# Routing logits and norm sums inside the output projection, and a gather for four experts at a time

## The reference

```python
x = x + merged @ w_out[l]
x = x + expert_choice_ffn(rms_norm(x, norm_ffn[l]), router[l], exp_gate[l], exp_up[l], exp_down[l])

def expert_choice_ffn(h, router, w_gate, w_up, w_down):
    cap = CAPACITY_FACTOR * S // N_EXPERTS                       # 2 * 256 // 16 = 32
    aff = jax.nn.softmax(jnp.einsum('bsd,de->bse', h, router), axis=-1)
    vals, idx = lax.top_k(aff.transpose(0, 2, 1), cap)
    xg = jax.vmap(lambda hb, ib: hb[ib])(h, idx)
    hid = jax.nn.silu(jnp.einsum('becd,edf->becf', xg, w_gate)) * jnp.einsum('becd,edf->becf', xg, w_up)
    y = jnp.einsum('becf,efd->becd', hid, w_down) * vals[..., None]
    return ...                                                   # y added at the chosen tokens
```

## Time and profile before

| | us |
|---|---|
| median of 3 runs | 1902.39 (1899.36 to 1904.59) |
| the profiled execution | 1904.66 |
| its span | 1902.9 |
| PE busy in the span | 1573.6 (83%) |
| weight load busy | 1152.3 (61%) |
| DVE busy | 549.2 (29%) |
| ACT busy | 259.3 (14%) |
| DMA | 405.39 MB, 213 GB/s over the span |

### The profile page before, as it was taken

One profiled execution on the slowest core, in us unless ns is written; L12 is line 12 of the kernel. 1 busy time (PEld: TensorE's weight loads), 2 busy tenths in 40 slices (PEclk: granted clock), 3 DMA queues, 4 the chain that ended last, 5 costly groups with the idle time before them and its releaser, 6 DMA issues.

```text
span 1902.9 us, 25312 instructions
## 1 busy us (share of the span) xinstructions
PE 1573.6 (83%) x11140; PEld 1152.3 (61%) x11140; DVE 549.2 (29%) x1199; ACT 259.3 (14%) x618; POOL 72.0 (4%) x96
## 2 busy tenths in 40 slices
PE   7979999998879999999878879998866656666666
PEld 4857788886637888878656657776732222222223
DVE  3670444301132311033647554323220000000002
ACT  2330100002212000001323222220100000000001
POOL 0120000000000000000110111200000000000000
PEclk8989999998979999999988999999988787778787
DMA  8466578744343644333100001323629999999992
GB/s 359 155 258 248 218 279 318 278 142 155 133 155 121 236 151 155 138 128 133 68 24 24 2 24 45 114 108 126 250 87 421 422 420 421 421 421 420 419 421 105
DMA packets 57485, 405.39 MB, mean 213 GB/s; under 512 B 6168, under 2 KB 8344, under 8 KB 8864
## 3 DMA queue, kind: packets, MB, share of 16 engines
q1 hardware_dynamic: 53984, 390.35, 52.5%
q10 hardware_dynamic: 3392, 13.42, 1.8%
HBM read 402.69 MB, written 1.06 MB: 212 GB/s over the span
## 4 chain that ended last, share of the span: by engine, by line
PE 65%; DMA 23%; DVE 9%; ACT 2%; issue 1%; POOL 0%; ACTq 0%; SPq 0%; POOLq 0%; DVEq 0%
PE bank L409 63%; DMA weight_ring<-weights 22%; DVE arena L1499 3%; PE bank L416 2%; DVE arena L1505 2%; ACT arena L1151 1%; DVE arena L1502 1%; DVE arena L1830 1%; DVE rstd L1555 1%; DVE normed_T L1505 0%; DMA arena<-x 0%; DVE rstd L1897 0%; DVE arena L1692 0%; DVE arena L1828 0%; ACT normed_T L1151 0%
## 5 line engine op out<-in xcount | busy, mean ns | idle before, releaser
L409 PE MATMUL bank<-normed_T,weight_ring 128*128 128x256 f32 x2640 | 608.1, 388 | 27.0 <-ACT arena L1151 12.4
L409 PEld LDWEIGHTS bank<-normed_T,weight_ring 128*128 128x128 f32 x2640 | 504.5, 194 | 108.1 <-ACT arena L1151 18.0
L409 PE MATMUL bank<-weight_ring,arena 128*32 128x256 f32 (+1 forms) x2976 | 270.0, 484 | 146.9 <-DMA weight_ring<-weights 138.5
L409 PE MATMUL bank<-arena,weight_ring 128*128 128x256 f32 x1456 | 329.6, 384 | 9.7 <-ACT arena L1151 6.8
L409 PEld LDWEIGHTS bank<-arena,weight_ring 128*128 128x128 f32 x1456 | 279.5, 193 | 51.0 <-issue 8.5
L409 PEld LDWEIGHTS bank<-weight_ring,arena 128*32 128x32 f32 (+1 forms) x2976 | 100.7, 132 | 302.9 <-DMA weight_ring<-weights 206.5
L1151 ACT ACTIVATE arena<-bank 128x256 f32<-128x256 f32 (+4 forms) x299 | 109.9, 374 | 1171.2 <-PE bank L409 625.1
L409 PE MATMUL bank<-arena 64*64 64x64 f32 (+7 forms) x3096 | 225.7, 283 | 28.4 <-DVE arena L1499 14.1
L409 PEld LDWEIGHTS bank<-arena 64*64 64x64 f32 (+5 forms) x3096 | 167.3, 155 | 97.5 <-issue 48.6
L1505 DVE SCALAR_TENSOR_TENSOR arena<-arena,bank 128x256 f32<-128x256 f32 x141 | 59.4, 422 | 544.1 <-PE bank L409 276.4
L416 PE MATMUL bank<-packed_consts,arena 128*128 128x128 f32 (+1 forms) x166 | 42.8, 358 | 65.1 <-DVE arena L1502 35.6
(11 more groups left out here) (119 smaller groups left out, 637.5 us busy)
## 6 DMA issues: line engine op xcount, KB each, us to landing
weight_ring<-weights SPq DMA_DIRECT2D x370, 1024.0 KB, 10.2
arena<-ahead ACTq DMA_DIRECT2D x8, 1024.0 KB, 18.0
packed_consts<-packed ACTq DMA_DIRECT2D x1, 2852.0 KB, 13.6
arena<-bias_by_distance ACTq DMA_DIRECT2D x2, 1024.0 KB, 7.0
arena<-x SPq DMA_DIRECT2D x1, 1024.0 KB, 5.2
out<-arena SPq DMA_DIRECT2D x2, 512.0 KB, 2.6
packed_consts<-packed SPq DMA_DIRECT2D x1, 254.5 KB, 2.8
bias_by_distance<-arena ACTq DMA_DIRECT2D x1, 16.0 KB
```

Source lines behind the costliest of these rows:

```text
L409: return e.matmul(out, lhsT, rhs, start=start, stop=stop, skip_group_check=True)
```

## The change

- w_out is written out with `route_sums(n)` after the next block. DVE no longer waits for the norm: after each residual block it multiplies it by the norm's weight alone (`ts`) into hT. ACT's squares go to an area `sq8` of their own. `route_sums` makes four products for a block: two of 16 columns (logits of the tokens of each half, not yet divided by the norm) and two of one column (sums of squares per token).
- The norm is now a number per token on its partition. ACT takes the root of two 128x1 columns, loads the table of the exponential, and takes the exponentials with the reciprocal of the root as scale; the copies to htok multiply by it too.
- PE's transposes of hT come after w_out; three of the four clears of accumulators come between the transposes of the affinities and the places, the fourth after the gather.
- DVE's first round of the top tokens reads the bank directly; the copies and the subtraction of 1 go, and the iota starts at 1.
- The selection is made for a group of four experts at a time (128 columns). Group 0 is gathered before the experts, with 16 products of 128 columns, into B[2] and B[3]; group g + 1 in two halves of 8 products into B[3], after the mixes of the second and the third expert of group g, with an ACT copy each. `gsel` goes; `g4` is computed for each expert from places and affinities.

The lines added, with a little around them (what is removed stands in the functions above):

```diff
 EXPERTS, CAP = 16, 32
+BATCH = 4
+BATCHES = EXPERTS // BATCH
...
+ROUTE_PE = {"sum": 2, "aff": 3, "place": 4}
+ROUTE_V = {"bias": 1, "aff": 2, "place": 3, "select": 4}
...
+        self.sel = a.take(NT * EXPERTS * CAP)
+        self.xg = [a.take(KD * BATCH * CAP) for _ in range(2)]
+        self.sq8 = area[:, NT * D:NT * D + KD * T]
+        self.aff, self.post, self.st = a.take(NT * EXPERTS), a.take(NT * EXPERTS), a.take(6 * NT)
+        self.wk, self.mk, self.ps_ = [a.take(T)[0:EXPERTS, :] for _ in range(3)]
...
+        self.zeros = a.take(P)
...
+        a = Arena(area, n, a.at)
...
+    def route_sums(n):
+
+        e.wait_ge(s.normed, 8 * NORM_FFN2 + n + 1)
+        for j in range(NT):
+            ins = mm(B[6 + j][:, 0:EXPERTS], hT[:, n, j * P:(j + 1) * P], m.col("router", n * EXPERTS, EXPERTS), n == 0, n == KD - 1)
+            if n == KD - 1:
+                ins.then_inc(s.route_pe, 1)
+        e.wait_ge(s.square, squares_before(NORM_FFN2) + n + 1)
+        for j in range(NT):
+            ins = mm(B[4 + j][:, 0:1], m.sq8[:, n * T + j * P:n * T + (j + 1) * P], m.ones[:, 0:1], n == 0, n == KD - 1)
+        if n == KD - 1:
+            ins.then_inc(s.sumsq, 1)
+
+    for n in range(KD):
         if n < 4:
             e.wait_ge(s.branch_out, 2 * KD + n + 5)
...
+        else:
+            e.wait_ge(s.xT, 8 * NORM_FFN2 + n - 3)
+        for k in range(KD):
+            if n == 0:
+                e.wait_ge(s.merged, k + 1)
+            w = feed.tile("w_out_2", k, n)
+            if k < KD - 1:
+                fed(B[n % 4][:, 0:T], w, m.mg[:, k, :], k == 0, False)
+            else:
+                mm(B[n % 4][:, 0:T], w, m.mg[:, k, :], False, True).then_inc(s.res, 1)
+        if n:
+            route_sums(n - 1)
+    route_sums(KD - 1)
...
     e.wait_ge(s.xT, 8 * NORM_FFN2 + KD)
...
+    e.wait_ge(s.route_v, ROUTE_V["aff"])
+    e.wait_ge(s.root, NORM_FFN2 + 1)
     for j in range(NT):
         ins = flip(B[4][0:EXPERTS, j * P:(j + 1) * P], m.aff[:, j * EXPERTS:(j + 1) * EXPERTS])
     ins.then_inc(s.route_pe, 1)
...
+    e.wait_ge(s.zeroed, ZEROED["experts"])
+    for j in range(1, 4):
+        mm(B[4 + j][:, :], m.zeros, m.hT_[:, 0:512], True, False)
+    e.wait_ge(s.route_v, ROUTE_V["place"])
     for j in range(NT):
         ins = flip(B[4][:, j * EXPERTS:(j + 1) * EXPERTS], m.ps_[:, j * P:(j + 1) * P])
     ins.then_inc(s.route_pe, 1)
...
+
+    def gather(g, k, out):
+
+        for j in range(NT):
+            at = j * EXPERTS * CAP + g * BATCH * CAP
+            ins = mm(out, m.htok[:, j, k * P:(k + 1) * P], m.sel[:, at:at + BATCH * CAP], j == 0, j == NT - 1)
+        return ins
+
+    e.wait_ge(s.route_v, ROUTE_V["select"])
     e.wait_ge(s.h_tok, 2 * NT)
...
+    for half in range(2):
+        for k in range(4):
+            ins = gather(0, 4 * half + k, B[2 + half][:, k * P:(k + 1) * P])
         ins.then_inc(s.x_sum, 1)
...
+    e.wait_ge(s.route_v, ROUTE_V["select"] + 1)
+    mm(B[4][:, :], m.zeros, m.hT_[:, 0:512], True, False)
     for x in range(EXPERTS):
...
+        g, y = x // BATCH, x % BATCH
+        xg = [m.xg[g % 2][:, k * P + y * CAP:k * P + (y + 1) * CAP] for k in range(KD)]
+        if y == 0:
+            e.wait_ge(s.x_out, 2 * g + 2)
         if x:
             e.wait_ge(s.e_act, x)
         quarters(B[0], f"exp_gate{x}", lambda k: xg[k]).then_inc(s.e_gate, 1)
...
+        e.wait_ge(s.x_out, 2 * g + 2 + max(0, y - 1) * (g + 1 < BATCHES))
...
+        if y in (1, 2) and g + 1 < BATCHES:
+            e.wait_ge(s.route_v, ROUTE_V["select"] + g + 1)
+            for k in range(4):
+                ins = gather(g + 1, 4 * (y - 1) + k, B[3][:, k * P:(k + 1) * P])
+            ins.then_inc(s.x_sum, 1)
...
     e.wait_ge(s.o_out, 2 * n_items)
     for c in range(AHEAD):
         e.dma_start(m.ahead[:, c * TPC * P:(c + 1) * TPC * P], dram["ahead"][c]).then_inc(s.ahead[c], 16)
...
+    for n in range(KD):
+        e.wait_ge(s.xT, 8 * NORM_FFN2 + n + 1)
+        act(m.sq8[:, n * T:(n + 1) * T], xT[:, n, :], ACT.Square).then_inc(s.square, 1)
+        if n == 0:
+            e.preload_act_table(ACT.Sqrt)
+    e.wait_ge(s.sumsq, NORM_FFN2)
+    for j in range(NT):
+        ins = act(m.st[:, j:j + 1], B[4 + j][:, 0:1], ACT.Sqrt, scale=1.0 / D, bias=m.col("eps"))
+    ins.then_inc(s.root, 1)
+    e.preload_act_table(ACT.Exp)
+    e.wait_ge(s.route_v, ROUTE_V["bias"])
+    for j in range(NT):
+        act(m.aff[:, j * EXPERTS:(j + 1) * EXPERTS], B[6 + j][:, 0:EXPERTS], ACT.Exp, scale=m.st[:, j:j + 1], bias=m.st[:, 4 + j:5 + j],
+            accum_out=m.st[:, 6 + j:7 + j]).then_inc(s.route_exp, 1)
     for j in range(NT):
         for q in range(2):
             e.wait_ge(s.h_flip, 2 * j + q + 1)
...
+            act(m.htok[:, j, q * 512:(q + 1) * 512], B[2 * j + q][:, :], ACT.Copy, scale=m.st[:, j:j + 1]).then_inc(s.h_tok, 1)
+
+    def gathered(g, half, bank):
+        e.wait_ge(s.x_sum, 2 * g + half + 1)
+        act(m.xg[g % 2][:, half * 512:(half + 1) * 512], bank[:, :], ACT.Copy).then_inc(s.x_out, 1)
+
+    for half in range(2):
+        gathered(0, half, B[2 + half])
...
+        if x % BATCH in (1, 2) and x // BATCH + 1 < BATCHES:
+            gathered(x // BATCH + 1, x % BATCH - 1, B[3])
 
...
+    for n in range(KD):
+        e.wait_ge(s.res, next(res_done))
+        stt(xT[:, n, :], B[n % 4][:, 0:T], 0.5, xT[:, n, :], ALU.mult, ALU.add).then_inc(s.xT, 1)
+        e.wait_ge(s.xT, 8 * NORM_FFN2 + n + 1)
+        ts(hT[:, n, :], xT[:, n, :], col("norm_ffn_2", n), None, ALU.mult).then_inc(s.normed, 1)
+    st = m.st
+    rstd, top, bias, total = [st[:, j * NT:(j + 1) * NT] for j in range(4)]
+    affs = tiles(m.aff, EXPERTS)
     for j in range(NT):
...
+        e.wait_ge(s.route_pe, j + 1)
+        ins = e.tensor_reduce(top[:, j:j + 1], B[6 + j][:, 0:EXPERTS], AX, ALU.max)
+    link(ins)
+    e.wait_ge(s.root, NORM_FFN2 + 1)
+    link(e.reciprocal(rstd, rstd))
+    link.wait()
+    stt(bias, top, -1.0, rstd, ALU.mult, ALU.mult).then_inc(s.route_v, 1)
+    e.wait_ge(s.route_exp, NT)
+    link(e.reciprocal(total, total))
+    link.wait()
+    tt(affs, affs, total.unsqueeze(2).to_broadcast([P, NT, EXPERTS]), ALU.mult).then_inc(s.route_v, 1)
+    e.wait_ge(s.route_pe, ROUTE_PE["aff"])
+    for i in range(CAP // 8):
+        left = m.wk if i else B[4][0:EXPERTS, 0:T]
+        if i:
+            link.wait()
+        link(e.max(m.m8, left))
         link.wait()
...
+        link(e.match_replace(out=m.wk, in_to_replace=m.m8, in_values=left, imm_value=-1.0))
     link.wait()
     link(ts(m.mk, m.wk, 0.0, None, ALU.is_lt))
     link.wait()
     link(e.tensor_tensor_scan(m.ps_, m.mk, col("zero")[0:EXPERTS, :].to_broadcast([EXPERTS, T]), 0.0, ALU.add, ALU.add))
     link.wait()
...
+    tt(m.ps_, m.ps_, m.mk, ALU.mult).then_inc(s.route_v, 1)
+    selv = m.sel.rearrange("p (m e c) -> p m e c", m=NT, e=EXPERTS)
+    def select(g, place):
+        mine = slice(g * BATCH, (g + 1) * BATCH)
+        for j in range(NT):
+            ins = tt(selv[:, j, mine, :], tiles(place, EXPERTS)[:, j, mine].unsqueeze(2).to_broadcast([P, BATCH, CAP]),
+                     col("iota", 0, CAP).unsqueeze(1).to_broadcast([P, BATCH, CAP]), ALU.is_equal)
+        ins.then_inc(s.route_v, 1)
+    e.wait_ge(s.route_pe, ROUTE_PE["place"])
+    select(0, B[4][:, 0:NT * EXPERTS])
+    link(e.tensor_copy(m.post, B[4][:, 0:NT * EXPERTS]))
     link.wait()
...
     for x in range(EXPERTS):
         if x:
             e.wait_ge(s.g_flip, x)
         for j in range(NT):
...
+            at = j * EXPERTS + x
+            ins = ts(tiles(m.g4[:, j * P:(j + 1) * P], CAP), col("iota", 0, CAP).unsqueeze(1).to_broadcast([P, 4, CAP]),
+                     m.post[:, at:at + 1], m.aff[:, at:at + 1], ALU.is_equal, ALU.mult)
         ins.then_inc(s.g4, 1)
+        if x + 1 < BATCHES:
+            select(x + 1, m.post)
         e.wait_ge(s.e_tanh, x + 1)
         stt(m.act_, m.act_, 1.0, B[0][:, 0:QW], ALU.add, ALU.mult).then_inc(s.e_act, 1)
         e.wait_ge(s.e_up, x + 1)
...
+    e.wait_ge(s.normed, 8 * NORM_FFN2 + KD)...
+    c["iota"] = np.tile(np.arange(1, CAP + 1, dtype=np.float32), (P, 1))
```

More of the change, by code:

```diff
@@ L155 @@
 FIRST_V = {"silu": 1, "decay_consts": 2}
-ROUTE_PE = {"sum": 0, "aff": 2, "place": 3}
-ROUTE_V = {"max": 0, "aff": 2, "affT": 3, "place": 4, "placeT": 5, "select": 6}
+ROUTE_PE = {"sum": 2, "aff": 3, "place": 4}
+ROUTE_V = {"bias": 1, "aff": 2, "place": 3, "select": 4}
 class Signals:
@@ L1061, in tensor_program @@
             ins.then_inc(s.h_flip, 1)
-    e.wait_ge(s.branch_out, 3 * KD)
-    e.wait_ge(s.yb, KR)
-    for j in range(NT):
-        for k in range(KD):
-            ins = mm(B[6 + j][:, 0:EXPERTS], hT[:, k, j * P:(j + 1) * P], m.col("router", k * EXPERTS, EXPERTS), k == 0, k == KD - 1)
-        ins.then_inc(s.route_pe, 1)
-    e.wait_ge(s.route_v, ROUTE_V["aff"] + 1)
+    e.wait_ge(s.route_v, ROUTE_V["aff"])
+    e.wait_ge(s.root, NORM_FFN2 + 1)
     for j in range(NT):
@@ L1452, in scalar_program @@
```

(46 more changed lines are left out.)

53 lines of the change are left out of this document (2 added, 51 removed).

## The result

| | before | after |
|---|---|---|
| median, us | 1900.95 (1899.36 to 1904.59, 4 runs) | 1873.59 (1871.53 to 1874.88, 4 runs) |
| the profiled execution | 1904.66 | 1874.88 |
| its span | 1902.9 | 1873.1 |

The change makes the kernel 27.4 us faster: the ratio is 0.9853, with an interval of 0.9838 to 0.9869. The prediction was 1876 (1869 to 1883). Of the 2.4 us between it and the result, 1.4 are the median of the kernel before, which a fourth run moved from the 1902.39 that the prediction started from to 1900.95.

The account below looks back on a forecast made before the run. The expert weight stream, restarted by the first expert product, was taken to bound the kernel. Gains of 8.4 + 1.1 + 2.4 + 14.3 = 26.2 us ahead of that product gave 1876 us for the median, range 1869 to 1883.

Parts of the forecast that it names:

- The view of the whole: Expert stage: weight stream restarts at the first expert product, runs 449 us without a gap; moving that product moves the end equally.
- Inside w_out: Output columns of w_out: four thin products replace the norm product, 0.42 us more a column, w_out ends 2.5 us later.
- To the affinities' transposes: Routing, from w_out's last residual update to the transposes of the affinities: these come 8.4 us earlier, w_out's 2.5 us cost included.
- Top tokens and selection: Routing before the gather: dropped copies and subtraction gain 1.1 us, selection by two 128x128 operations gains 2.4 us.
- The gather: Gather's start to first expert product: 16 products of 128 columns, then copy and clear, 6.8 for 21.1 us, gain 14.3.
- In the expert stage: Six half gathers, their copies and three selections moved into the expert stage are hidden by PE's waits and the ring.
- Booked 0: Cost taken for the gathers moved into the expert stage; without cover they would cost 20 us.
- rivals B and C: Expert stage hand-overs: B, gathers break the stream, 20 us back, 1896, chance 0.04; C, experts lengthen, 31 us, 1907, chance 0.02.
- six chunks of lead are 15 us: Expert stage: argument against a slower kernel, that chunks waiting in the ring let the stream catch longer hand-overs.
- Tail: After the weight stream's end: work untouched, but PE's clock phase may move it by up to 3 us either way.

## Why the prediction was right

**The view of the whole** held: the stage as long as before (453.6 us both times), its start set by the first expert product, the end moved by as much. The end of the stream of before was read 1.3 us late, which changes no term of the sum. The run with twelve more clears (10.3 us in, 9.9 out) and the run with three fewer streamed chunks show it from both sides.

**Inside w_out.** Updates are 4.35 us apart, 4.31 were forecast. The sum is 2.8 us for 2.5: the four thin products take 4 x 0.223 us in a block, not 4 x 0.213. The price of 128x1 products from another stage carried over to 128x16 ones.

**To the affinities' transposes.** From the last update it is 1.96 us to the roots (1.9 forecast), 2.39 to the load of the table (2.45), 3.69 to the exponential (3.75) and 4.97 to the transposes (5.0). The two roots, of a shape that the trace of before didn't have, take 0.41 us together where 0.54 was booked; the exponentials are 0.36 apart as assumed. The transposes of the tokens took 1.95 us, at full clock, and ended at 1373.6, ahead of the affinities: no part of the path.

**Top tokens and selection.** 1.3 and 2.6 us for 1.1 and 2.4. MAX from a bank took 0.42 us, the same as from SBUF, as the value chosen had it.

**The gather.** 14.9 us for 14.3. The clock was the open question: I took the 4.9 us after the start at which it had come back before. It came back after 3.3 us (0.66 over the stretch to 1385: half speed for 3.4 us, from 1381.4 to 1384.8). The 5.40 us are inside the bounds of 3.4 and 6.9. The run with more clears shows what all products at full clock take, 3.84: the 0.215 us for one, a quarter of a product of 512 columns, was too low. And 11.5 products at 0.43 us and 4.5 at 0.215 are 5.9 us, where the prediction has 5.8.

**In the expert stage: right, for a reason that was wrong.** "Booked 0" held within 0.3 us. But the cover that the prediction named, 9 us of PE's waits an expert and up to six chunks in the ring, "15 us of lead", is no sum that can be spent. PE's waits lie between chunks and can't be saved up, and the ring has five slots to give from the moment at which PE is level with the stream. The true cover is 8.7 us at a hand-over. The absences in the changed kernel are 4.7 to 7.6 us: the last down chunk and its copy 1.6 or 2.5, then mix and half gather 3.1 at full clock, up to 5.1 at half. Its longest, from PE's timeline:

```profile
1439.42 1.94 PE L410 MATMUL bank<-weight_ring,arena 128*32 128x256 f32 x16 [1.42 <-DMA weight_ring<-weights]
1441.90 5.18 PE L410 MATMUL bank<-arena 32*128 32x256 f32 x32 [0.55 <-DVE arena L2154]
1447.01 3.66 PE L410 MATMUL bank<-weight_ring,arena 128*32 128x256 f32 x64
```

From 1439.42 to 1447.01 it is 7.6 us, 1.1 short of the limit. One half gather more at each place (run with the products twice) is already over it twice. That nothing was lost is luck to this extent. So the step that failed is the size of the cover, and rivals B and C were nearer than their argument "six chunks of lead are 15 us" made them: not 20 or 31 us, but a loss that begins at 8.7 us of absence. PE's waits for weights did fall, from 133.9 us to this, by about the 14 us that the six half gathers took (us in total, times, longest; 1400 to 1836 us):

```profile
PE bank L410 <- DMA weight_ring<-weights: 117.7, 115, 2.4
```

**Tail.** The 3 us either way were real: it fell by 2.5 us here, and with eight chunks on the chip it lies between 31.8 and 35.7 us in the profiles.

## What to carry over

When a stage is bound by a stream, find the event that restarts it and sum only what stands ahead of that event. As the runs with more gather products show, work moved into the stage is free only if each single absence of the consumer fits into the buffer's free slots, less the way of a chunk and the restart; an engine's total of idle time says nothing on that, and many short pieces are safe where one long one isn't. And price a step with its likely clock: keeping the engine busy just before it can shorten it by more than the extra work costs, as the head shows here (1.6 us), though no median does.

## What was not expected of the hardware

- The stream outlives 8.7 us of PE's absence with five free slots of 1 MB, not 12.5: it stops 10.5 us after the last chunk that PE begins on arrival, and moves again 1.75 us after a slot is freed.
- Four fp32 products with 128x128 weights, two of 16 columns and two of 1, cost 0.89 us between wide ones, much as four of 1 column (0.85). So the number of columns doesn't set it; that the load of the weights does is likely, but no run isolates it.
- With 12.7 us more of PE's work in each of six experts, spread, the stream got 0.5 us longer, and PE's mean clock over the whole execution was higher, 0.931 for 0.909.
